# Loading the last down-projection's weights early and turning its loops around in an eight-core decoder-trunk kernel

## What is computed

```python
def rmsnorm(x, g):
    xf = x.astype(jnp.float32)
    r = lax.rsqrt(jnp.mean(xf * xf, axis=-1, keepdims=True) + RMS_EPS)
    return (xf * r).astype(x.dtype) * g

def macaron_half_ffn(x, g, wg, wu, wd):
    h = rmsnorm(x, g)
    return x + 0.5 * ((jax.nn.silu(h @ wg) * (h @ wu)) @ wd)

# per group (prompt, sample): D_MODEL = 1024, D_FF = 2816
y = macaron_half_ffn(y, *ffn1)
...   # mixer: windowed attention beside an S5 state-space block, output projection added to y
y = macaron_half_ffn(y, *ffn2)
y = rmsnorm(y, final_norm)
```

## Time and profile before

| | us |
|---|---|
| median of 2 runs | 1671.82 (1670.71 to 1672.92) |
| the profiled execution, device time | 1671.24 |
| its span on the slowest core, core 7 | 1669.7 |
| spans of the eight cores | 1656.7 to 1669.7 |
| TensorE matmul busy on core 7 | 1394.8 |
| VectorE / ScalarE / GpSimd busy | 630.7 / 445.9 / 186.0 |

### The profile page before, as it was taken

How to read it: one execution, slowest core, us unless ns; L and a number is a source line. 1 busy time by engine, 2 the same in 40 slices (tenths; PEclk the granted TensorE clock), 3 DMA queues, 4 the chain that set the end, 5 groups by cost and what they waited for, 6 DMA issues and landing times.

```text
span 1669.7 us, 20816 instructions; the slowest of 8 cores (1656.7 to 1669.7 us)
## 1 busy us (share of the span) xinstructions
PE 1394.8 (84%) x7382; PEld 616.5 (37%) x7382; DVE 630.7 (38%) x1164; ACT 445.9 (27%) x790; POOL 186.0 (11%) x277
## 2 busy tenths in 40 slices
PE   1799999999997769995466546876999999999994
PEld 0244444444443325331122113332444444444441
DVE  1422254433265452113866761335222222212226
ACT  2513100131100062675353423124111001111014
POOL 0000000000000001004555550000000000000000
PEclk9999999999998869997577657997999999999997
DMA  7342222222121103000000002120222122221215
GB/s 187 116 63 53 35 36 47 39 46 39 31 42 23 14 6 44 8 1 0 1 1 0 1 1 57 26 39 13 39 39 35 30 45 39 39 38 31 36 18 208
DMA packets 41780, 65.19 MB, mean 39 GB/s; under 512 B 16904, under 2 KB 21800, under 8 KB 41648
## 3 DMA queue, kind: packets, MB, share of 16 engines
q0 software_dynamic: 23072, 41.20, 15.9%
q1 hardware_dynamic: 18608, 22.67, 4.5%
HBM read 95.90 MB, written 11.17 MB: 64 GB/s over the span
## 4 chain that ended last, share of the span: by engine, by line
PE 74%; DVE 8%; issue 7%; ACT 6%; DMA 3%; POOL 2%; DVEq 0%; ACTq 0%; SPq 0%; POOLq 0%
PE ps L299 19%; PE ps L304 19%; PE ps L344 18%; PE ps L844 3%; DMA xT_s<-xT 3%; PE ps L1335 2%; PE ps L548 2%; PE ps L238 2%; ACT sq L234 2%; PE ps L524 1%; DVE hT_s L259 1%; DVE xT_s L253 1%; PE ps L1341 1%; POOL hT_s L1270 1%; PE ps L1213 1%
## 5 line engine op out<-in xcount | busy, mean ns | idle before, releaser
L299 PE MATMUL ps<-hT_s,ws 128*128 128x512 bf16 (+1 forms) x1760 | 352.9, 344 | 2.1 <-DVE xT_s L348 2.0
L304 PE MATMUL ps<-hT_s,ws 128*128 128x512 bf16 (+1 forms) x1760 | 351.1, 342 | 0.0
L344 PE MATMUL ps<-aT_s,ws 128*128 128x512 bf16 (+1 forms) x1760 | 328.2, 349 | 0.0
L313 DVE TENSOR_TENSOR aT_s<-ps,sg 128x512 bf16<-128x512 f32 (+1 forms) x220 | 131.1, 598 | 460.6 <-PE ps L304 440.5
L310 ACT ACTIVATE sg<-ps 128x512 f32<-128x512 f32 (+1 forms) x220 | 114.9, 523 | 594.8 <-PE ps L299 588.5
L299 PEld LDWEIGHTS ps<-hT_s,ws 128*128 128x128 bf16 x1760 | 151.5, 98 | 170.6 <-issue 6.0
L344 PEld LDWEIGHTS ps<-aT_s,ws 128*128 128x128 bf16 x1760 | 150.9, 100 | 170.1 <-issue 12.9
L304 PEld LDWEIGHTS ps<-hT_s,ws 128*128 128x128 bf16 x1760 | 151.3, 98 | 167.3 <-issue 2.1
L348 DVE SCALAR_TENSOR_TENSOR xT_s<-ps,xT_s 128x512 f32<-128x512 f32 (+1 forms) x160 | 94.1, 596 | 182.6 <-PE ps L344 182.3
L234 ACT ACTIVATE sq<-xT_s 128x512 bf16<-128x512 f32 (+1 forms) x160 | 81.1, 547 | 284.4 <-PE ps L238 224.8
L238 PE MATMUL ps<-sq,ones_s 128*128 128x512 bf16 (+1 forms) x160 | 65.9, 437 | 94.3 <-ACT sq L234 91.2
(11 more groups left out here) (282 smaller groups left out, 1079.0 us busy)
## 6 DMA issues: line engine op xcount, KB each, us to landing
ws<-wgu POOLq DMA_DIRECT2D x44, 512.0 KB, 5.2
ws<-wd POOLq DMA_DIRECT2D x32, 352.0 KB, 4.5
xT_s<-xT SPq DMA_DIRECT2D x4, 2048.0 KB, 21.9
yT<-xT_s SPq DMA_DIRECT2D x4, 2048.0 KB, 7.3
ws<-win POOLq DMA_DIRECT2D x9, 256.0 KB, 4.3
ws<-wout POOLq DMA_DIRECT2D x8, 256.0 KB, 4.3
stage_s<-scr_f SPq DMA_DIRECT2D x16, 64.0 KB, 3.6
ks<-cK_nat SPq DMA_DIRECT2D x1, 992.0 KB, 7.4
```

Of the source, the lines that this page charges most:

```text
L299: t_g = P.op('pe', lambda e, kc=kc, t0=t0, n=n, gps=gps, wv4=wv4: e.matmul(gps[:, :n], wv4[:, 0, kc, :], hT[:, kc, t0:t0 + n], start=(kc = ...
L304: t_u = P.op('pe', lambda e, kc=kc, t0=t0, n=n, ups=ups, wv4=wv4: e.matmul(ups[:, :n], wv4[:, 1, kc, :], hT[:, kc, t0:t0 + n], start=(kc = ...
L313: t_a = P.op('dve', lambda e, jj=jj, t0=t0, n=n, ups=ups, sg=sg: e.tensor_tensor(out=aT[:, jj, t0:t0 + n], in0=ups[:, :n], in1=sg[:, :n], ...
L344: t_y = P.op('pe', lambda e, jj=jj, t0=t0, n=n, yps=yps, wv3=wv3: e.matmul(yps[:, :n], wv3[:, jj, :], aT[:, jj, t0:t0 + n], start=(jj == 0 ...
```

## The change

It has three parts.

1. `mixer` keeps the token of its last matmul as `mix_end_tok`.
2. In `ffn`, for gi = 2, ahead of the down-projection of h = 0, POOL issues five loads: the down blocks c = 0 to 4 of round h = 1, into `stage` (two), `cKT`, `cV` and `BT`, each with a semaphore of its own, waiting for `mix_end_tok`.
3. For gi = 2, h = 1, the down-projection has a branch of its own. The blocks c = 5, 6, 7 are loaded through the ring; then the outer loop runs over the tiles and the inner one over the eight c. `final_tile(ti)` follows each tile. The old loop is skipped there.

```diff
+            if gi == 2 and h == 0 and getattr(self, "mix_end_tok", None) is not None and not self.debug.get("no_tail_opt"):
+                stb = self.stage[:].rearrange("p a h q -> p (a h q)").bitcast(BF16)
+                fl = lambda t: t[:].rearrange("p a b -> p (a b)")
+                bufs = [stb[:, 0:1408], stb[:, 2048:3456], fl(self.cKT)[:, 0:1408], fl(self.cV)[:, 0:1408],
+                        self.BT[:].rearrange("p a b c -> p (a b c)")[:, 0:1408]]
+                self.res_wd = []
+                for c_, bf in enumerate(bufs):
+                    tk = P.dma('pool', lambda e, bf=bf, c_=c_: e.dma_start(out=bf, in_=wd_d[1, c_].rearrange("p j n -> p (j n)")),
+                               self.slot("d_rwd%d" % c_), waits=[self.mix_end_tok])
+                    self.res_wd.append((bf.rearrange("p (j n) -> p j n", j=NJH), tk))
+            if gi == 2 and h == 1 and getattr(self, "res_wd", None):
+                chunks = list(self.res_wd)
+                ring = []
+                for c in range(5, KC):
+                    wv, t_w, wi = self.ws_load(wd_d[h, c].rearrange("p j n -> p (j n)"), lambda t: t[:, 0:NJH * 128])
+                    chunks.append((wv.rearrange("p (j n) -> p j n", j=NJH), t_w))
+                    ring.append(wi)
+                t_y = None
+                for ti, (t0, n) in enumerate(TT):
+                    for c in range(KC):
+                        wv3, t_w = chunks[c]
+                        yb = YB[ycnt % 4]
+                        ycnt += 1
+                        yps = self.ps[yb]
+                        for jj in range(NJH):
+                            t_y = P.op('pe', lambda e, jj=jj, t0=t0, n=n, yps=yps, wv3=wv3: e.matmul(
+                                yps[:, :n], wv3[:, jj, :], aT[:, jj, t0:t0 + n], start=(jj == 0), stop=(jj == NJH - 1)),
+                                waits=([t_w, self.ps_rd[yb]] if jj == 0 else []) + [tok_a[(jj, ti)]],
+                                signal=(jj == NJH - 1))
+                        t_x = P.op('dve', lambda e, c=c, t0=t0, n=n, yps=yps: e.scalar_tensor_tensor(
+                            out=xT[:, c, t0:t0 + n], in0=yps[:, :n], scalar=0.5, in1=xT[:, c, t0:t0 + n],
+                            op0=ALU.mult, op1=ALU.add),
+                            waits=[t_y, self.tok_x[(c, ti)]])
+                        self.tok_x[(c, ti)] = t_x
+                        self.ps_rd[yb] = t_x
+                    self.final_tile(ti)
+                for wi in ring:
+                    self.ws_release(wi, t_y)
+                self.aT_rd = t_y
+                continue
...
         self.sg_rd = [t_y, t_y]
+        self.mix_end_tok = t_y
```

## The result

The changed kernel takes 1664.16 us against 1672.24 us (medians of all runs). In some runs the cores of one die are granted a lower clock and the time is some per cent longer; without those the means are 1664.6 us and 1671.5 us, 6.9 us less, a ratio of 0.9959, 95% interval 0.9947 to 0.9970. A second set of runs, on another occasion, gave 0.9968 (0.9954 to 0.9981), 5.4 us less. The prediction had 3.9 us less, a ratio of 0.9977.

The account below looks back on a forecast made before the run. The loss was placed in the last column block's matmul groups alternating with final norms at VectorE's and ScalarE's pace. 94.5 (four large tiles) + 20.2 (end) + 1.6 (clock) = 116.3 us against 120.2 us, giving 1667.9 us, range 1663.5 to 1673 us.

Parts of the forecast that it names:

- no weight load was late: Last down-projection: TensorE busy for all of its first 71 us, so a prefetch alone brings nothing; early loads cost nothing.
- the scalings hide behind the next tile's groups: Large tiles: first PSUM bank free after 9.05 us, needed after 9.50 us, so scalings hide with 0.4 us to spare.
- the second wait: Old end piece, from the second tile: the c = 7 addition queues on VectorE behind eight scalings of the tile before.
- the short tile loses its cover: Short last tile: its fifth group waits for an addition behind the fourth tile's scalings; costs 4.2 us more, bounds 3.1 to 5.0.
- 7.1 + 4 x 0.6 us: Short tile: fifth group waits until 7.1 us after the fourth sum, then four groups of 0.6 us, ending at 9.6 us.
- the last output: Kernel's end: 5.6 us from the last short scaling to the end of the span, for issue and landing, carried over.
- The clock: Three gaps ahead of large tiles: low clock paid 1.1 times, 1.6 us each; one payment taken, bounds 0 to 4.8 us.
- The argument on scatter: Core 2 began its piece 1.4 us ahead of core 7, which speaks for one to two payments on the last core.
- rival 2: Gaps ahead of large tiles: none pays the low clock on the slowest core; 5.5 us less, 1666.3 us; chance 0.14.
- The gap: After each large tile's groups: squares and sums hand in hand, TensorE doing nothing else, 4.62 us per tile.
- Rival 1: Gaps ahead of large tiles: every one pays the low clock; 0.8 us less than before, 1671.0 us; chance 0.2.
- Rival 3: After gaps, the low clock stays longer under dense work; 5.0 us more, 1676.8 us; decides from 1.8 us per gap; chance 0.08.

Follow-up runs that it names:

- prefetch_only: Changed kernel's early loads kept, but the last down-projection's loops as before (block outside, tile inside); ratio to the kernel before 1.0021 (1.0000 to 1.0043).
- old_order_defer: Kernel before, no early loads or new loop order, each tile's eight scalings put behind the next tile's addition; second set of runs: ratio 0.9977 (0.9966 to 0.9988).
- before_no_out3: Kernel before with the fourth tile's output left out; one time, 1671.56 us, last phase 117.9 to 118.2 us.
- after_short_early: Changed kernel with the short tile's eight groups and additions ahead of the fourth tile's norm; ratio to before 0.9966 (0.9954 to 0.9979).
- after_long_gap: Changed kernel with three extra squares per final norm on ScalarE, making the gaps 6.80 us; last phase 126.6 to 127.4 us on six cores.

## Why the prediction was right in its build and small in its size

*That no weight load was late, and the early loads cost and bring nothing.* Right: prefetch_only, and 236.5 us between the two down-projections in both profiles.

*That the scalings hide behind the next tile's groups.* Right, with the 0.4 us to spare never used up: each tile's 88 matmuls are one piece of 19.0 us, also the second tile's, which runs beside the norm with ScalarE's table load.

*That the scalings ahead of the next addition were the second wait.* Right: old_order_defer took them away in the old order and each gap fell to 4.5 us.

*That the short tile loses its cover.* Right in its mechanism and nearly in its size: the first addition came 7.0 us behind the fourth sum (6.9 predicted), the last sum ended 12.5 us behind it (12.1). On the way the prediction's 7.1 + 4 x 0.6 us is 9.5 us, not 9.6 us; it changes nothing.

The sum was 116.3 us, the slowest core had 112.4 us. Of the 3.9 us between them 0.6 us are the gaps, 1.6 us the clock and 2.2 us the last output, less 0.4 us by which the short tile was longer:

| term of the sum | predicted, us | measured, us |
|---|---|---|
| four gaps | 4 x 4.62 | 4 x 4.48 |
| payments of the clock, slowest core | 1.6 | 0 |
| fourth sum, after the start | 96.1 | 93.9 |
| last short scaling to the end | 5.6 | 3.45 |
| from the fourth sum to the end | 20.2 | 18.5 |

*The last output.* This is the largest miss of mechanism. I carried the 5.6 us from before over as a fixed cost "for the issue and landing of the last output". It held 2.2 us of collision with the fourth tile's output, issued 3.4 us ahead of it, while a 2 MB output takes 7.3 us to land. before_no_out3 showed it. I had even written that the outputs leave a tile apart and called that "not on the path"; the last one was on it.

*The clock.* I took one payment for the core that ends last, from three payments in eight first gaps, and argued that scatter between cores would favour a core that paid. Three in eight was a fair rate for the old order's first gap (16 of 48 with the variants), but it did not carry over: the new order's gaps paid 12 times in 72, so 0.5 times per core and not 1.1 times. The argument on scatter was wrong as well: the cores begin the phase up to 16 us apart, ten times the price of a payment, and in eleven of the twelve profiles the last core to begin it is the slowest. Whether that one has paid is then chance, about even here. It paid in neither profile of the changed kernel, and in that of after_short_early it did. The unpaid case was rival 2, and it is the one that came; that it came in both profiles is luck.

*The gap.* The 4.62 us were taken on a core that paid, where the last sums already ran at the low level. Cores of before that kept the clock had 4.48 us.

Rival 1 (every gap pays) fell on the count. Rival 3, the slower case, had its point at 1.8 us per gap; the most seen after a gap of 4.48 us was 1.5 us, and on core 0 the clock was back at 1.00 by 1620 us, some three microseconds after dense work began again. At 6.8 us every gap pays, and there it is 1.0 to 1.5 us each.

What made the gain, on the chain's own count from 120.2 to 112.4 us: the fourth sum ends 10.3 us earlier. Of these 2.2 us are seven short groups that were only moved, 5.0 us are shorter gaps (22.9 us in all on core 7 before, 17.9 us now), and 3.1 us the clock that core 7 had paid after its first two gaps. Behind the fourth sum it is 18.5 us where it was 16.0 us: the last output brings 2.2 us, so the waiting short tile gives back 4.7 us.

## What to carry to other kernels

A fixed piece at a kernel's end, read off as "last instruction to end", may hold a collision: look at what else is on the DMA engines there before carrying it over. A loop order that puts a reduction and a scaling behind each tile is improved more by dealing them out between the next tile's matmul groups (17.6 us here) than by turning the loops alone, so that the waits come after more work (5 to 7 us). And where cores start a phase further apart than the effect in question, count the effect per core, and take the late starter as the slowest, not the unlucky one. A rate counted at one place of a kernel need not hold at another, even for a gap of the same length.

## What the runs showed of the hardware that was not expected

In after_long_gap cores 2 and 3, both of the first four, showed a granted clock of 0.81 for 73 and 76 us of the phase, from 34 us after its start. It is neither of the two levels that every other core of the twelve profiles has. Stretches of core 2:

```profile
1577.00:1580.00 3.00, 2.95 (x14) 1.36 (x14) 3.00 (x5) 0.00 (x0) 0.00 (x0) 1.00 0.00 0
...
1583.00:1586.00 3.00, 3.00 (x14) 1.21 (x12) 0.69 (x1) 0.00 (x0) 0.00 (x0) 0.81 1.04 365
...
1611.00:1614.00 3.00, 3.00 (x13) 1.28 (x12) 0.69 (x1) 0.00 (x0) 0.00 (x0) 0.81 1.03 375
```

A group of 11 matmuls took 2.89 us there (start to start, 1611.81 to 1614.70 us) against 2.375 us: the ratio is 0.82. Their phase was 137.7 and 138.4 us against 126.6 to 127.4 us on the other six. The Trainium skill (TensorE: Matmul & The Clock Gate, "Part 1: The HAM clock gate (the "warmup" mystery)") has a peak-current limit of 13/16 for a whole die once three of its cores run dense matmuls. The 0.81 agrees with 13/16; the rest does not: all eight cores run dense matmuls at 1.00 in every profile (1549 to 1620 us of core 7 before, for one), and only two of the four cores show 0.81 in this one. What set it off was not tried.

The landing of an output depends on its company: 256 KB took 2.8 us alone, 5.0 us with one 2 MB output 3.4 us ahead, and 8.5 us behind several; 2 MB took 7.2 us alone and 9.5 us among others (medians of old_order_defer2, core 4). Company is not all of it: the fourth tile's 2 MB of the changed kernel took 8.4 to 8.8 us with none of its core's outputs ahead of it, and why was not tried.
